# Two heads at a time in two attentions: paired matmuls, weights scaled on GpSimd, gate sums spread by DMA

## The chip, the cores and the metric

The kernel runs on one core of a Trainium2 chip. The metric is the device time of one execution in microseconds (us), taken as the median of several runs. The engines are named as the profile names them: PE (TensorE matmuls), PEld (its weight loads), DVE (VectorE), ACT (ScalarE), POOL (GpSimd), SP (SyncE, which issues all DMAs here).

## The reference

A token sequence of 256 rows of 1024 goes through two blocks: a first one of two layers (a mixer and a squared-ReLU MLP each) and a second one of one hybrid layer (SwiGLU, attention and state-space mixer, SwiGLU). The change touches the mixers of the first block's two layers only.

Layer 0 (called "even" in the kernel): 8 heads of block attention and 8 heads (2 groups of 4) of an attention with three branches, compressed keys, selected keys and window, that are weighted with gates and added. At 256 tokens both kinds of selection cover all keys, so each head is a causal softmax with a bias that depends on the distance:

```python
s = einsum('hqd,hkd->hqk', q, k) * 64**-0.5 + bias[h, bucket(t_q - t_k)]
o = einsum('hqk,hkd->hqd', masked_softmax(s, t_k <= t_q), v)     # nsa heads: g1 * slc + g2 * win + g0 * cmp
```

Layer 1 ("odd"): 16 heads of an attention with a forgetting gate:

```python
log_f = log_sigmoid(fz + b_forget)
cum = cumsum(log_f, axis=1).transpose(0, 2, 1)                   # per head
s = einsum('bhqd,bhkd->bhqk', qc, k) * scale + cq[..., None] - cum[:, :, None, :]
p = masked_softmax(s, key_pos[None, :] <= t[:, None])
o = einsum('bhqk,bhkd->bhqd', p, v)
```

## The kernel before

**Weights.** All weights come as a stream of 1 MB chunks from HBM in the order of use (`fetch_to`, issued by SP into three buffers RAW). ACT rounds a chunk to its high part WH (`hi_to`, L572), DVE subtracts to get the low part WL (`lo_to`, L580), and PE multiplies with both. `sp_gemm`, `act_gemm`, `dve_gemm` walk the products of the network in one fixed order, about two chunks ahead of PE. Every engine has its own hand-written program; semaphores join them. SP may load a RAW buffer again once WL of the chunk three places back is made.

**One attention step.** Layer 0 has 24 softmax passes over heads (8, then 8 selected and 8 window passes; called heads here), layer 1 has 16. Each engine runs a loop over i, and the stages of one head lie on different steps:

- PE, step i: the scores of head i (`pe_even_scores` L1363 and L1364, `pe_odd_scores` L1650 to L1659): queries in two tiles of 128, the first against 128 keys, the second against 256, so 384 columns in one PSUM bank. A head has 64 channels, so this product uses 64 of the 128 partitions; even heads lie on partitions 0 to 63, odd heads on 64 to 127. In layer 1 the gate's sums (`o_ln`, SPL, `trir`) and the causal mask are added by further matmuls into the same bank.
- DVE, step i: in layer 0 one custom instruction per query tile adds the bias from `e_bt` and finds the maximum (`dve_max_biased`, L909, L910). In layer 1 two plain maxima (L925, L926) and two small operations with the sums CQ (L1596, L1598).
- ACT, step i: exponential with row sum (`act_exp_biased` L899, L900, or `act_exp` L889, L890) into PB, four buffers.
- DVE, step i+1: reciprocal of the row sum (L934), and PB times it, in layer 0 times the gate too (`dve_weigh`, L941, L943).
- PE, step i+2: three transposes of PB (`pe_turn`, L879) into bank 5 or 6. ACT, step i+2: copy to PT, three buffers (`act_turned`, L918), which waits for the value product of the head before.
- PE, step i+3: the value product (`pe_pv`, L947, L948): 128 keys against the head's 64 columns of v, so output partitions 0 to 63 for even heads and 64 to 127 for odd ones. In layer 0 L1393 adds the compressed branch.
- After two heads (four in the later part of layer 0) ACT and DVE write the output rows as high and low part (`act_out` L953, `dve_out` L957) for the output product eo or oo, which follows at once.

PE issues in the order of its program: in step i scores of i, transposes of i-2, values of i-3. Two chunks of eo (at ACT steps 10 and 16, DVE steps 11 and 17) and of oo (5 and 10, 6 and 11) are split inside the loops.

**Around them.** In layer 0 the product ev1 stands in PE's program at step 2, the gates are computed on DVE at step 4, and four transposes of the compressed weights come at PE's step 6. In layer 1 the order of products is oq, ok, ov0, ov1 and then the attention; the gate's running sums are made by three small matmuls after ok and copied to CQ by DVE (L1584).

## Time and profile before

| what | value |
|---|---|
| median of 3 runs | 1335.26 us (1331.81 to 1339.88) |
| profiled execution, its own time | 1341.18 us |
| its span | 1339.4 us |
| PE busy | 1276.9 us, 95% |
| DVE busy | 859.8 us, 64% |
| ACT busy | 664.0 us, 50% |
| POOL busy | 197.1 us, 15% |
| attention of layer 0, after ev1 | 118.96 to 177.59, 58.63 us |
| attention of layer 1 | 456.96 to 505.60, 48.64 us |

Times are microseconds from the start of the span. The two last lines are stretches between instructions of PE: from its first score matmul after ev1 (or after ov1) to the first matmul of the output product. A matmul of two fp32 operands appears as two instructions ("x2"). Its end is modelled, so starts are the safer reading: what a matmul costs in a full queue is the distance from its start to the next start.

### The profile page before, as it was taken

The numbers are of one execution on the slowest core, as the hardware profiler recorded it, in microseconds if no ns is written. First come the engines' busy times: TensorE is split into PE (matmuls) and PEld (weight loads), VectorE is DVE, ScalarE is ACT, GpSimd is POOL, SyncE is SP. The second block draws the span as 40 slices with busy tenths as digits, with TensorE's granted clock in tenths as the row PEclk, the third lists the DMA queues.
The fourth block names the chain that finished last, engine by engine and source line by source line (L and its number), as shares of the span: only waits on it lengthen the run. The fifth ranks groups of instructions, "written<-read, shape, count | busy, mean of one in ns | idle before, by whom it ended". The sixth has DMA issues, their size and how long they took to land.

```text
span 1339.4 us, 19395 instructions
## 1 busy us (share of the span) xinstructions
PE 1276.9 (95%) x7812; PEld 1099.7 (82%) x7812; DVE 859.8 (64%) x1359; ACT 664.0 (50%) x1081; POOL 197.1 (15%) x224
## 2 busy tenths in 40 slices
PE   5999999999999999999999999999899889999996
PEld 5877578888888767888888888998897569888896
DVE  5864757666568376766557776547765665867643
ACT  5324646663333365665445554435544544655531
POOL 4000011120000001111111221101303401111201
PEclk8988999999999999999999999999899969999999
DMA  6590115555455212556554554562351005355461
GB/s 259 188 267 33 64 64 188 183 185 199 159 193 189 90 64 95 189 188 220 189 189 153 187 187 157 195 222 95 128 198 48 1 22 207 122 193 186 142 207 64
DMA packets 33913, 204.52 MB, mean 153 GB/s; under 512 B 3744, under 2 KB 6304, under 8 KB 13728
## 3 DMA queue, kind: packets, MB, share of 16 engines
q1 hardware_dynamic: 33824, 203.28, 43.9%
q8 instruction: 62, 1.02, 0.3%
q14 instruction: 27, 0.22, 0.1%
HBM read 201.82 MB, written 1.44 MB: 152 GB/s over the span
## 4 chain that ended last, share of the span: by engine, by line
PE 79%; DVE 12%; ACT 4%; DMA 2%; issue 1%; POOL 1%; SPq 1%; POOLq 0%; ACTq 0%; DVEq 0%
PE ps L636 32%; PE ps L641 22%; PE ps L639 6%; PE ps L640 6%; DVE wl L580 4%; PE ps L947 2%; PE ps L660 1%; PE ps L661 1%; PE ps L662 1%; DMA raw<-wstream 1%; ACT wh L572 1%; DVE xb L714 1%; ACT xb L694 1%; PE ps L948 1%; DVE y L1858 1%
## 5 line engine op out<-in xcount | busy, mean ns | idle before, releaser
L580 DVE TENSOR_TENSOR wl<-raw,wh 128x2048 fp32r<-128x2048 f32 (+3 forms) x201 | 435.6, 2173 | 149.4 <-ACT wh L572 148.8
L636 PE MATMUL ps<-xb,wh 128*128 128x512 f32 x1424 | 504.1, 399 | 4.6 <-DVE wl L580 3.5
L641 PE MATMUL ps<-xb,wl 128*128 128x256 f32 x1712 | 485.1, 283 | 0.0
L572 ACT ACTIVATE wh<-raw 128x2048 fp32r<-128x2048 f32 (+3 forms) x201 | 358.0, 1784 | 163.6 <-PE ps L641 124.3
L641 PEld LDWEIGHTS ps<-xb,wl 128*128 128x128 f32 x1712 | 328.8, 192 | 0.0
L636 PEld LDWEIGHTS ps<-xb,wh 128*128 128x128 f32 x1424 | 268.7, 189 | 71.4 <-issue 7.6
L641 PE MATMUL ps<-ab,wl 128*128 128x256 f32 x1088 | 307.6, 283 | 0.0
L636 PE MATMUL ps<-ab,wh 128*128 128x512 f32 x640 | 225.1, 397 | 2.7 <-DVE wl L580 2.7
L641 PEld LDWEIGHTS ps<-ab,wl 128*128 128x128 f32 x1088 | 207.6, 191 | 0.0
L636 PEld LDWEIGHTS ps<-ab,wh 128*128 128x128 f32 x640 | 120.2, 188 | 32.2 <-issue 2.2
L833 DVE TENSOR_TENSOR tf<-ps,tf 128x256 f32<-128x256 f32 x148 | 61.9, 421 | 118.2 <-ACT tf L828 118.2
L828 ACT ACTIVATE tf<-ps 128x256 f32<-128x256 f32 x148 | 56.3, 383 | 149.8 <-PE ps L641 148.2
L639 PE MATMUL ps<-ab,wh 128*128 128x256 f32 x448 | 128.3, 286 | 0.0
L640 PE MATMUL ps<-ab,wh 128*128 128x256 f32 x448 | 127.9, 285 | 0.0
L639 PE MATMUL ps<-xb,wh 128*128 128x256 f32 x288 | 85.4, 297 | 22.2 <-DVE wl L580 9.3
L724 POOL TENSOR_TENSOR acc<-acc,sq 128x256 f32<-128x256 f32 x42 | 30.7, 739 | 466.0 <-ACT sq L705 465.2
L639 PEld LDWEIGHTS ps<-ab,wh 128*128 128x128 f32 x448 | 86.5, 193 | 0.2
L640 PEld LDWEIGHTS ps<-ab,wh 128*128 128x128 f32 x448 | 86.5, 193 | 0.1
L1722 POOL TENSOR_TENSOR tf<-sg,tf 128x256 f32<-128x256 f32 x44 | 53.0, 1207 | 213.7 <-ACT sg L1687 213.7
L640 PE MATMUL ps<-xb,wh 128*128 128x256 f32 x288 | 84.3, 293 | 0.0
L639 PEld LDWEIGHTS ps<-xb,wh 128*128 128x128 f32 x288 | 58.2, 202 | 23.4 <-issue 9.9
L694 ACT ACTIVATE xb<-h,vecs 128x256 fp32r<-128x256 f32 x48 | 24.0, 508 | 78.9 <-DVE h L1471 37.6
(336 smaller groups left out, 1476.0 us busy)
## 6 DMA issues: line engine op xcount, KB each, us to landing
raw<-wstream SPq DMA_DIRECT2D x157, 1024.0 KB, 4.8
raw<-wstream SPq DMA_DIRECT2D x32, 704.0 KB, 4.1
raw<-wstream SPq DMA_DIRECT2D x8, 768.0 KB, 4.3
e_bt<-scratch SPq DMA_DIRECT2D x16, 128.0 KB, 6.3
raw<-wstream SPq DMA_DIRECT2D x2, 560.0 KB, 10.0
raw<-wstream SPq DMA_DIRECT2D x4, 256.0 KB, 5.6
h<-xt SPq DMA_DIRECT2D x4, 256.0 KB, 5.8
raw<-wstream SPq DMA_DIRECT2D x2, 512.0 KB, 7.7
```

Of the source, the lines that this page charges most:

```text
L572: e.g.activation(WH[i % HLN][:, 0:w], RAW[i % RAWN][:, 0:w], ACT.Copy).then_inc(S["hi"], 1)
L580: e.g.tensor_tensor(WL[q][:, 0:w], RAW[i % RAWN][:, 0:w], f32(WH[q][:, 0:w]), ALU.subtract).then_inc(S["lo"], 1)
L636: e.g.matmul(PS[b][:, :].rearrange("p (a t) -> p a t", a=2), wh[:, sl], x2[:, :, cs], start=start, stop=k == p.nk - 1, skip_group_check=pair)
L639: e.g.matmul(o, wh[:, sl], xh[:, cs], start=start, stop=False, skip_group_check=pair)
L640: e.g.matmul(o, wh[:, sl], xl[:, cs], start=False, stop=False, skip_group_check=pair)
L641: ins = e.g.matmul(o, wl[:, sl], xh[:, cs], start=False, stop=k == p.nk - 1, skip_group_check=pair)
L694: e.g.activation(XH[:, tile(k)], H[:, tile(k)], ACT.Copy, scale=gain(n, k)).then_inc(S["xh"], 1)
L724: e.g.tensor_tensor(acc, acc, SQ[:, mth * T:mth * T + T], ALU.add).then_inc(S["acc"], 1)
L828: e.g.activation(o, PS[p.bank[u]][:, T:2 * T], ACT.Copy).then_inc(S["low"], 1)
L833: return e.g.tensor_tensor(o, PS[p.bank[u]][:, 0:T], o, ALU.add)
L947: e.g.matmul(o[:, 0:256], v0, pt[:, 0:256], start=start, stop=False)
L1722: e.g.tensor_tensor(TF[j % 4][:, 0:T], SG[j % 2][:, :], TF[j % 4][:, T:2 * T], ALU.mult).then_inc(S["gp"], 1)
```

## The change

- Scores of two heads are issued together, in turn: the 128-column product of both, then the 256-column product of both. A fourth score bank (2) is added. PE issues them at odd steps, for heads i+1 and i+2.
- Value products of two heads are issued in turn, both into one bank, at even steps for heads i-4 and i-3. The banks of outputs are now two instead of three. In layer 0 the selected passes of both groups now come before the window passes of both.
- PB is scaled by POOL (`pool_weigh`) instead of DVE. DVE keeps the reciprocal.
- The copies of transposed weights are divided: even heads ACT, odd heads DVE (`dve_turned`). They wait for the value product three heads back instead of one.
- Layer 1: the running sums go as 16 rows of 256 into TMP, by DMA to a scratch in HBM, and come back by two DMAs that spread them over 128 partitions (`o_bt`, 1 MB each). DVE adds them with the maximum, as in layer 0. The matmuls of L1656 and L1659, and DVE's L1596 and L1598, go. SP waits for the sums before it issues the fetches of ov1.

```diff
+        o_bt = [place("o_bt0", 8 * T, at=ra), place("o_bt1", 8 * T, at=rl)]
...
+        def turned(j):
+
+            return (S["ptd" if j % 2 else "pt"], j // 2 + 1) if j < 40 else (S["pt"], j - 20 + 1)
...
-                e.wait_ge(S["pt"], j - len(A.TB) + 1)
+                e.wait(turned(j - len(A.TB)))
...
-            if i >= 3:
-                e.wait_ge(S["wt"], A.base + i - 3 + 1)
...
-            if j > A.pv_base:
-                e.wait_ge(S["pv"], j)
+            if j >= 3:
+                e.wait_ge(S["pv"], j - 3 + 1)
             e.g.activation(PT[j % 3][:, :], PS[A.turn_bank(q)][:, 0:384], ACT.Copy).then_inc(S["pt"], 1)
...
+        def dve_turned(e, A, q):
+            j = A.pv(q)
+            e.wait_ge(S["tp"], j + 1)
+            if j >= 3:
+                e.wait_ge(S["pv"], j - 3 + 1)
+            e.g.tensor_copy(PT[j % 3][:, :], PS[A.turn_bank(q)][:, 0:384]).then_inc(S["ptd"], 1)
+
+        def dve_reciprocal(e, A, q):
+
+            e.wait_ge(S["ex"], A.base + q + 1)
+            e.g.reciprocal(rs(q), sm(q)).then_inc(S["iv"], 1)
+
+        def pool_weigh(e, A, q, no, gate=None):
+            p, r = PB[q % 4], rs(q)
+            e.wait_ge(S["iv"], no + 1)
+            for tb, s in ((0, slice(0, 128)), (1, slice(128, 384))):
+                ins = e.g.tensor_scalar(p[:, s], p[:, s], r[:, tb:tb + 1], gate(tb) if gate else 1.0, ALU.mult, ALU.mult)
+            ins.then_inc(S["wt"], 1)
 
...
-        EVEN = Attention(0, 24, (3, 4, MISC), (5, 6), 0)
+        EVEN = Attention(0, 24, (3, 4, MISC, 2), (5, 6), 0)
...
+            for i in range(EVEN.n):
+                if i == 8:
+                    e.wait_ge(S["gated"], 2)
+                pool_weigh(e, EVEN, i, i, even_gate(i))
...
-                if 0 <= i - 2 < A.n:
+                if 0 <= i - 2 < A.n and i % 2 == 0:
                     act_turned(e, A, i - 2)
...
-            return d % 3
+            return d % 2
...
-                    dve_inverse(e, A, i - 1)
-                    dve_weigh(e, A, i - 1, even_gate(i - 1))
+                    dve_reciprocal(e, A, i - 1)
+                if 0 <= i - 2 < A.n and i % 2:
+                    dve_turned(e, A, i - 2)
...
+            pe_even_scores(e, 0)
             for i in range(A.n + 3):
...
+                    e.wait_ge(S["ol"], 1)
                     e.wait_ge(S["pct"], 2)
...
-                if i < A.n:
-                    pe_even_scores(e, i)
+                if i % 2 and i + 1 < A.n:
+                    pe_even_scores(e, i + 1)
                 if 0 <= i - 2 < A.n:
                     if i - 2 < 2:
...
-                if 0 <= i - 3 < A.n:
-                    pe_even_pv(e, i - 3)
+                if i % 2 == 0 and 0 <= i - 4 < A.n:
+                    pe_even_pv(e, i - 4)
...
+            if i == 2:
+                e.wait(G["even"].free.get(2))
+            if i >= 4:
                 e.wait_ge(S["mx"], i - 3 + 1)
...
+            for at, n in ((0, 128), (128, 256)):
+                for par in range(2):
+                    p_, ps = slice(64 * par, 64 * par + 64), PS[A.bank(i + par)]
+                    ins = e.g.matmul(ps[:, at:at + n], q[p_, qt + at:qt + at + 128], k[p_, kt:kt + n], start=True, stop=True)
+                    if at:
+                        ins.then_inc(S["sc"], 1)
...
-            if d < 3:
+            if d < 2:
                 e.wait(G["even"].free.get(b))
             else:
-                e.wait_ge(S["ol"], d - 3 + 1)
+                e.wait_ge(S["ol"], d - 2 + 1)
             if d == 2:
                 e.wait_ge(S["ptc"], 1)
-            e.wait_ge(S["pt"], q + 1)
-            pt = PT[q % 3]
+            for x in range(2):
+                e.wait(turned(q + x))
...
+                    for x in range(2):
+                        e.g.matmul(o[x][:, 0:256], e_vc[32 * j:32 * j + 32, 64 * x:64 * x + 64],
+                                   e_ptc[x][32 * j:32 * j + 32, :], start=True, stop=False)
...
+            for x in range(2):
+                e.g.matmul(o[x][:, 0:256], e_v[0][:, at[x]:at[x] + 64], pt[x][:, 0:256], start=start, stop=False)
+            for x in range(2):
+                e.g.matmul(o[x][:, 128:256], e_v[1][:, at[x]:at[x] + 64], pt[x][:, 256:384], start=False,
+                           stop=stop).then_inc(S["pv"], 1)
...
-        ODD = Attention(24, 16, (3, 4, MISC), (5, 6), 24)
+        ODD = Attention(24, 16, (3, 4, MISC, 2), (5, 6), 24)
 
         def sp_odd(e):
-            for name in ("on", "oq", "ok", "ov0", "ov1", "oo"):
+            for name in ("on", "oq", "ok"):
                 sp_gemm(e, G[name])
+            e.wait_ge(S["bt0"], 128)
+            e.wait_ge(S["bt1"], 128)
+            e.wait_ge(S["cq"], 1)
+            e.g.dma_start(bass.AP(scratch.tensor, 0, [[T, 16], [1, T]]), TMP[1][0:16, 0:T]).then_inc(S["d_scr"], 16)
+            sp_gemm(e, G["ov0"])
+            e.wait_ge(S["d_scr"], 32)
+            for i in range(2):
+                src = bass.AP(scratch.tensor, i * 8 * T, [[0, 128], [1, 8 * T]])
+                e.g.dma_start(o_bt[i][:, :], src).then_inc(S[f"ct{i}"], 16)
+            sp_gemm(e, G["ov1"])
+            sp_gemm(e, G["oo"])
...
-                    act_exp(e, A, i)
-                if 0 <= i - 2 < A.n:
+                    act_exp_biased(e, A, i)
+                if 0 <= i - 2 < A.n and i % 2 == 0:
                     act_turned(e, A, i - 2)
...
-            e.wait_ge(S["lf"], 1)
-            e.link(e.g.tensor_scalar(o_ln[:, :], o_lf[:, :], -1.0, None, ALU.mult))
-            e.settle()
-            e.link(e.g.tensor_copy(SPL[:, 0:16], o_ln[:, 0:16]))
-            e.settle()
-            e.g.tensor_tensor(SPL[:, 16:32], o_ln[:, 0:16], f32(SPL[:, 0:16]), ALU.subtract).then_inc(S["spl"], 1)
             dve_gemm(e, G["ok"], 0, drain=dve_to(G["ok"], o_k, 2))
             e.wait_ge(S["cum"], 1)
-            e.g.tensor_copy(CQ[:, 0:32], PS[MISC][:, 0:32]).then_inc(S["cq"], 1)
+            e.g.tensor_scalar(TMP[1][0:16, 0:T], PS[MISC][0:16, 0:T], -1.0, None, ALU.mult).then_inc(S["cq"], 1)
...
-                    cc, s = CQ[:, i:i + 32:16], SMALL[:, 64 + 2 * (i % 4):66 + 2 * (i % 4)]
-                    dve_max(e, A, i, last=False)
-                    e.wait_ge(S["cq"], 1)
-                    e.settle()
-                    e.link(e.g.tensor_tensor(s, cc, nm(i), ALU.subtract))
-                    e.settle()
-                    e.g.tensor_tensor(nm(i), cc, s, ALU.subtract).then_inc(S["mx"], 1)
+                    at = i % 8 * T
+                    e.wait_ge(S[f"ct{i // 8}"], 16)
+                    dve_max_biased(e, A, i, o_bt[i // 8][:, at:at + 128], o_bt[i // 8][:, at:at + T])
                 if 0 <= i - 1 < A.n:
-                    dve_inverse(e, A, i - 1)
-                    dve_weigh(e, A, i - 1)
+                    dve_reciprocal(e, A, i - 1)
+                if 0 <= i - 2 < A.n and i % 2:
+                    dve_turned(e, A, i - 2)
...
-            e.g.matmul(o[:, 0:16], c_("tri"), o_lf[:, 0:16], start=True, stop=True)
-            e.g.matmul(o[:, 16:32], c_("ones"), o_lf[:, 0:16], start=True, stop=False)
-            e.g.matmul(o[:, 16:32], c_("tri"), o_lf[:, 16:32], start=False, stop=True).then_inc(S["cum"], 1)
+            e.g.matmul(o[0:16, 0:128], o_lf[:, 0:16], c_("tri"), start=True, stop=True)
+            e.g.matmul(o[0:16, 128:256], o_lf[:, 0:16], c_("ones"), start=True, stop=False)
+            e.g.matmul(o[0:16, 128:256], o_lf[:, 16:32], c_("tri"), start=False, stop=True).then_inc(S["cum"], 1)
...
+            pe_odd_scores(e, 0)
             for i in range(A.n + 3):
-                if i < A.n:
-                    pe_odd_scores(e, i)
+                if i % 2 and i + 1 < A.n:
...
+                q = i - 4
+                if i % 2 == 0 and 0 <= q < A.n:
...
+                    b = d % 2
+                    if d < 2:
...
+                    for x in range(2):
+                        e.wait(turned(A.base + q + x))
+                    pts = [PT[(A.base + q + x) % 3] for x in range(2)]
+                    for s, v, c in ((slice(0, 256), 0, slice(0, 256)), (slice(128, 256), 1, slice(256, 384))):
+                        for x in range(2):
+                            ins = e.g.matmul(PS[b][64 * x:64 * x + 64, s], o_v[v][:, 64 * (q + x):64 * (q + x) + 64],
+                                             pts[x][:, c], start=v == 0, stop=v == 1)
+                            if v:
+                                ins.then_inc(S["pv"], 1)
...
-            ps, p_, t0 = PS[A.bank(h)], slice(64 * (h % 2), 64 * (h % 2) + 64), (h // 2) * T
-            e.wait_ge(S["ex"], 24 if h < 3 else A.base + h - 3 + 1)
-            e.wait_ge(S["cq"], 1)
-            e.wait_ge(S["spl"], 1)
-            e.wait_ge(S["const"], 1)
-            e.wait(G["ok"].done(3))
...
-            e.g.matmul(ps[:, 256:384], o_ln[:, 16 + h:17 + h].broadcast_to([128, 128]), c_("tri"), start=False, stop=False,
-                       skip_group_check=True)
-            for x in (h, 16 + h):
-                ins = e.g.matmul(ps[:, 0:384], SPL[:, x:x + 1].broadcast_to([128, 128]), trir[:, :], start=False,
-                                 stop=x > h, skip_group_check=True)
-            ins.then_inc(S["sc"], 1)
+            if h == 0:
+                e.wait_ge(S["ex"], 24)
+                e.wait_ge(S["cq"], 1)
+                e.wait_ge(S["const"], 1)
+                e.wait(G["ok"].done(3))
+            if h == 2:
+                e.wait(G["odd"].free.get(2))
+            if h >= 4:
+                e.wait_ge(S["mx"], A.base + h - 3 + 1)
+            t0, ps = h // 2 * T, [PS[A.bank(h + x)] for x in range(2)]
+            for at, n in ((0, 128), (128, 256)):
+                for x in range(2):
+                    p_ = slice(64 * x, 64 * x + 64)
+                    e.g.matmul(ps[x][:, at:at + n], o_q[p_, t0 + at:t0 + at + 128], o_k[p_, t0:t0 + n], start=at == 0,
+                               stop=False, skip_group_check=True)
+            for x in range(2):
+                for at in (0, 256):
+                    ins = e.g.matmul(ps[x][:, at:at + 128], identb[:, :], maskqb[:, :], start=False, stop=at == 256,
+                                     skip_group_check=True)
+                ins.then_inc(S["sc"], 1)
...
+            for i in range(ODD.n):
+                pool_weigh(e, ODD, i, 24 + i)
```

On PE in layer 1, about head 4 (`ps3` to `ps7` are PSUM banks, `o_k`, `o_q` keys and queries, `pb` the weights to transpose, `pt` the transposed ones, `o_v0` and `o_v1` the values of the first and second 128 tokens), before:

```order
L1650 MATMUL ps4<-o_k_119,o_q_118 128x128
L1652 MATMUL ps4<-o_k_119,o_q_118 128x256
L1654 MATMUL ps4<-maskqb_65,identb_64 128x128
L1655 MATMUL ps4<-maskqb_65,identb_64 128x128
L1656 MATMUL ps4<-consts_61,o_ln_123 128x128
L1659 MATMUL ps4<-trir_62,spl_80 128x384 x2
L879 MATMUL ps6<-consts_61,pb1_85 128x128 x3
L947 MATMUL ps2<-pt1_89,o_v0_120 64x256
L948 MATMUL ps2<-pt1_89,o_v1_121 64x128
```

The same place in the changed kernel, where the lines have moved to L1706 (scores), L1710 (mask), L884 (transposes) and L1684 (values):

```order
L1706 MATMUL ps7<-o_k_119,o_q_118 128x128
L1706 MATMUL ps2<-o_k_119,o_q_118 128x128
L1706 MATMUL ps7<-o_k_119,o_q_118 128x256
L1706 MATMUL ps2<-o_k_119,o_q_118 128x256
L1710 MATMUL ps7<-maskqb_65,identb_64 128x128 x2
L1710 MATMUL ps2<-maskqb_65,identb_64 128x128 x2
L884 MATMUL ps6<-consts_61,pb3_87 128x128 x3
L884 MATMUL ps5<-consts_61,pb0_84 128x128 x3
L1684 MATMUL ps1<-pt2_90,o_v0_120 64x256
L1684 MATMUL ps1<-pt0_88,o_v0_120 64x256
L1684 MATMUL ps1<-pt2_90,o_v1_121 64x128
L1684 MATMUL ps1<-pt0_88,o_v1_121 64x128
```

One head's nine rows have become twelve rows for two heads: two score products, two sets of transposes and two value products stand side by side, and no gate sums are among them.

On DVE in layer 1 before, one step (`nm` the maxima, `rs` the reciprocals, `sm` the row sums):

```order
L925 TENSOR_REDUCE nm_74<-ps7 128x1
L926 TENSOR_REDUCE nm_74<-ps7 128x1
L1596 TENSOR_TENSOR small_79<-cq_78,nm_74 128x2
L1598 TENSOR_TENSOR nm_74<-cq_78,small_79 128x2
L934 RECIPROCAL rs_76<-sm_75 128x2
L943 TENSOR_SCALAR pb1_85<-pb1_85,rs_76 128x128
L943 TENSOR_SCALAR pb1_85<-pb1_85,rs_76 128x256
```

In the changed kernel, a step with an odd number (5) and the first rows of the next:

```order
L912 ISA pb1_85,nm_74<-ps4,o_bt0_122 128x128
L912 ISA nm_74 128x1
L913 ISA pb1_85,nm_74<-ps4,o_bt0_122 128x256
L913 ISA nm_74 128x1
L963 RECIPROCAL rs_76<-sm_75 128x2
L958 COPY pt0_88<-ps6 128x384
L979 TENSOR_TENSOR ab_60<-ps0,ab_60 128x256
L581 TENSOR_TENSOR wl0_55<-raw0_49,wh0_52 128x2048
L912 ISA pb2_86,nm_74<-ps7,o_bt0_122 128x128
```

The scaling of PB is gone from DVE, and a copy that waits for PE's transposes (L958) now stands ahead of the next head's maximum, as do the output row (L979) and, at this step, a chunk's low part (L581).

On SP, the issues from ok to oo in the changed kernel (`raw` the weight buffers):

```order
L560 DMA raw_49<-wstream 128x2048
L1536 DMA scratch<-tmp_98 16x256
L560 DMA raw_50<-wstream 128x2048
L560 DMA raw_51<-wstream 128x2048
L1541 DMA o_bt_122<-scratch 128x2048
L1541 DMA o_bt_123<-scratch 128x2048
L560 DMA raw_49<-wstream 128x2048
```

The first row is ov0's second chunk, the next two weight rows are ov1's, and the last is oo's first. Before, the weight rows followed each other with nothing between them.

## Rows read from the trace of the kernel before

**Rows 1.** The page, busy time of PE, its share and instructions.

```profile
PE 1276.9 (95%) x7812; PEld 1099.7 (82%) x7812; DVE 859.8 (64%) x1359; ACT 664.0 (50%) x1081; POOL 197.1 (15%) x224
```

**Rows 2.** Windows: length, busy us (and count) by engine, TensorE clock, DMA share.

```profile
118.96:177.59 58.63, 55.24 (x278) 31.90 (x276) 40.17 (x180) 38.00 (x125) 0.00 (x0) 1.00 0.11 37
456.96:505.60 48.64, 46.33 (x274) 30.98 (x273) 31.64 (x121) 27.48 (x91) 0.00 (x0) 1.00 0.13 44
```

**Rows 3.** Timeline of PE, layer 0: start, length, what.

```profile
150.78 0.55 PE L879 MATMUL ps<-consts,pb 128*128 128x128 f32 x3
151.26 0.64 PE L1393 MATMUL ps<-e_ptc,e_vc 32*64 32x256 f32 x2
151.83 0.65 PE L947 MATMUL ps<-pt,e_v 128*64 128x256 f32 x2
...
152.62 0.49 PE L1363 MATMUL ps<-e_ks,e_qn 64*128 64x128 f32 x2
...
153.47 0.55 PE L879 MATMUL ps<-consts,pb 128*128 128x128 f32 x3
```

**Rows 4.** Timeline of PE, layer 1.

```profile
468.35 0.49 PE L1650 MATMUL ps<-o_k,o_q 64*128 64x128 f32 x2
...
469.20 0.23 PE L1654 MATMUL ps<-maskqb,identb 128*128 128x128 bf16 x1
...
469.33 0.44 PE L1656 MATMUL ps<-consts,o_ln 128*128 128x128 f32 x2
...
469.95 0.49 PE L879 MATMUL ps<-consts,pb 128*128 128x128 f32 x3
```

**Rows 5.** Timeline of PE, first two heads of layer 0.

```profile
108.64 0.59 PE L1364 MATMUL ps<-e_km,e_qm 64*128 64x256 f32 x1
...
108.84 0.56 PE L1363 MATMUL ps<-e_km,e_qm 64*128 64x128 f32 x1
...
109.41 1.06 PE L1364 MATMUL ps<-e_km,e_qm 64*128 64x256 f32 x2
110.39 0.60 PE L660 MATMUL ps<-wh,xb 128*128 128x280 f32 x1
```

**Rows 6.** Timelines of DVE and ACT, layer 0, start and length.

```profile
150.89 0.29 DVE L909 CUSTOM_DVE_ANT_0 pb<-ps,e_bt 128x128 f32<-128x128 f32 x1 [0.69 <-PE ps L1364]
...
151.57 0.40 ACT L899 ACTIVATE pb<-pb,nm 128x128 f32<-128x128 f32 x1 [0.49 <-DVE nm L910]
...
111.40 0.40 ACT L899 ACTIVATE pb<-pb,nm 128x128 f32<-128x128 f32 x1 [0.25 <-DVE nm L910]
...
112.42 0.17 DVE L934 RECIPROCAL rs<-sm 128x2 f32<-128x2 f32 x1 [0.49 <-ACT pb L900]
```

**Rows 7.** Single lines of POOL and ACT: count, ns min/median/max, first and last start.

```profile
L2033 POOL TENSOR_SCALAR tf<-m_u,vecs x12: 472/480/651, 928.1 to 957.2; 128x256 f32<-128x256 f32 x12
...
L1018 POOL CAST trir<-consts x3: 289/293/293, 28.8 to 29.3; 128x128 fp32r<-128x128 f32 x3
...
L918 ACT ACTIVATE pt<-ps x48: 465/487/517, 121.6 to 1089.7; 128x384 f32<-128x384 f32 x48
```

**Rows 8.** Timelines of ACT and DVE, chunk splits in layer 1.

```profile
469.83 1.93 ACT L572 ACTIVATE wh<-raw 128x2048 fp32r<-128x2048 f32 x1
...
472.07 2.28 DVE L580 TENSOR_TENSOR wl<-raw,wh 128x2048 fp32r<-128x2048 f32 x1
```

**Rows 9.** Before layer 1's attention: DVE, ACT, and all L559 fetches to landing.

```profile
435.68 0.18 DVE L1584 COPY cq<-ps 128x32 f32<-128x32 f32 x1
...
446.19 1.27 ACT L839 ACTIVATE o_v<-ps,rb 128x512 f32<-128x512 f32 x2 [3.46 <-PE ps L662]
...
DMA to landing us min/median/max: 1.8/4.8/11.7
```

**Rows 10.** Windows, as in Rows 2.

```profile
108.70:112.10 3.40, 3.40 (x16) 2.75 (x15) 2.75 (x15) 1.31 (x5) 0.00 (x0) 0.50 0.00 0
...
1064.40:1067.80 3.40, 0.85 (x5) 0.47 (x4) 3.31 (x7) 2.71 (x11) 2.16 (x3) 1.00 0.00 0
1067.80:1071.20 3.40, 3.40 (x11) 1.72 (x9) 0.24 (x2) 0.00 (x0) 2.12 (x3) 0.50 0.02 5
```

69 lines of the change are left out of this document (24 added, 45 removed).

## The prediction

> **What bounds the kernel now.** I read the page first: PE is busy for 95% of the span [rows 1], so a stage gets shorter only if PE's work or PE's waits there do. The windows of the two attentions come next: PE is busy for 55.24 of 58.63 us and for 46.33 of 48.64 us at the full clock, DVE for 40.17 and 31.64, ACT for 38.00 and 27.48, POOL not at all [rows 2]. Both stretches are PE's queue, and they are all that the change can shorten, 107.3 us in all. Third, the timeline of PE prices one head, from start to next start. Layer 0: transposes 0.48, compressed branch 0.57 (once for two heads), values 0.79, scores 0.85 [rows 3]; so 2.12 us a head without the branch and 2.69 with it. Layer 1: scores 0.85, masks 0.13, gate sums 0.62 [rows 4], with transposes and values 2.87 us a head. The reader is to see that nothing stands between these rows: each engine behind PE has slack.
>
> **What the change removes.** The gate sums go: 16 x 0.62 = 9.9 us of PE. The scores of two heads lie on different halves of the partitions. The trace has one place where two such products meet, the first two heads [rows 5]: head 1's 128 columns start at 108.84, 0.20 after head 0's 256 columns (108.64), and head 1's 256 columns start at 109.41. The clock is 0.50 there, 1.2 GHz [rows 10]. Head 1's 256 columns, alone, then take 0.98 us (109.41 to 110.39), so head 0's must have run from 108.64 to about 109.6, and head 1's 128 columns ran wholly beside them. Two halves do run at once. A pair therefore costs between 0.85 (all beside each other) and 1.70 (one after the other); I take 1.00, near the lower end, since the row shows a full overlap after 0.20 us. For value products, which split the output partitions and share all 128 input rows, no row shows two of them together: between 0.79 and 1.58 a pair; I take 0.95, by nearness to the scores. The Trainium skill (TensorE: Matmul & The Clock Gate, Part 3) states that column tiles run at once as row tiles do, with 2.38 times the rate for three; by it the value pair would be about 0.8 us, and rival B below would have no chance. No run here shows it, so B keeps one.
>
> **What PE then needs.** Layer 1, a pair: 1.00 + masks 0.26 + transposes 0.96 + values 0.95 = 3.17 us instead of 5.74. Layer 0: 2.91, and 3.24 where the branch comes (0.65 once in two pairs), instead of 4.24 and 4.81.
>
> **What waits instead.** With PE that fast I follow one round of the queues. DVE's copy of an odd head's transposed weights now stands ahead of the next head's maximum. From the start of the transposes of head h-3: transposes 0.50 with the handoff; copy 0.49 [rows 7]; output row, two thirds of that, 0.33; then head h's maximum, 0.68 from its start to that of the exponential (150.89 to 151.57) and 1.02 from there to the reciprocal (111.40 to 112.42) [rows 6]; reciprocal and handoff 0.22; POOL's scaling; then head h's transposes. POOL has no such instruction in the trace. The nearest rows are its tensor-scalar of 256 columns, 0.48, and its cast of 128, 0.29 [rows 7]: 0.77, and 0.87 with the handoff. Below this POOL can't go by any row; as upper end I take twice that, 1.5. Sum 4.11 us. Then PE does, in its order, head h's transposes, a value pair and a score pair (layer 1: 0.48 + 0.95 + 1.26 = 2.69) before the transposes of head h+1, with which the round repeats two pairs on. So two pairs take 6.80, a pair 3.40 us, a little more than PE's 3.17. In layer 0 the same sum, with the output row in half the rounds and the branch in half, gives 6.7, a pair 3.35. DVE (two maxima, two reciprocals, copy, row: about 2.3) and ACT (about 2.6) have room.
>
> **Chunk splits.** Each attention holds two: ACT 1.9 us, then DVE 2.3 us [rows 8]. Today PE's slack hides most. In the new round both engines are on the chain: the exponential, or the maximum behind the low part, comes late by the hi of 1.9 and the lo of 2.3 less gaps of about 1.3. I take 2.9 us of standstill for each of four splits; it is between 1 (hidden as now) and 4.2.
>
> **Layer 1.** Scores end at 456.96 + 1.26; first transposes 2.9 later, at 461.1; those of head 1 at 462.9 (0.48 + 1.26); head 15's seven pairs on, 486.7; transposes, copy and last value pair 2.1; splits 5.8: 494.6 instead of 505.60. **-11.0 us.** POOL, DVE and ACT here do everything beside PE. **Layer 0.** Up to head 6 the order is set by ev1, the gates on DVE (step 4) and the four transposes, now behind the first output row: 15.0 us today, 14.0 then. Eight periods 26.8, last pair 3.5, splits 5.8: 50.1 instead of 58.63. **-8.5 us.** The second score pair now ahead of ev1 only moves.
>
> **SP's queue.** The fetch of ov1's first chunk now stands behind the sums: DVE makes them at 435.7 [rows 9], with 256 columns instead of 32 until about 436.1, scratch write, issue at about 436.8, landing 4.8 later at the median, hi 1.8, lo 2.3: 445.7. PE needs it when ov0 ends, just before 446.19 [rows 9]. Cost 0; with the longest landing, 11.7, it is 6.5. I take 0.3. Behind it come ov1's second chunk (needed 5.5 us later) and the two 1 MB spreads; three more megabytes at 4.8 us each land by about 452 to 456, and DVE's first maximum needs them at 458.3: covered by ov1, but with 3 us or so to spare. What queues behind on SP is oo's first chunk, needed at step 5.
>
> **The clock.** After a stretch in which PE was busy 0.85 of 3.40 us the clock fell to half, 0.50 or 1.2 GHz [rows 10]. The four standstills of 2.9 us are of that kind. A pair under the lower clock takes twice PE's 3.17, 6.3 instead of 3.4 us: about 2.9 us for a fall that covers one pair. I take 2.4 falls (bounds 0 and 5): **+7.0 us**.
>
> **Sum.** -11.0 - 8.5 + 0.3 + 7.0 = -12.2 us against the profiled execution's 1341.18, so 1329.0. That execution was 5.9 us over the median of the runs (its span is 1339.4), so the median goes from 1335.3 to 1323.
>
> **Rivals.**
> A. The clock holds, or the splits hide better: -19 to -24 us, 1312 to 1316. For it: layer 0's loop is now at the full clock with PE busy for 94% [rows 2]. Against it: a standstill that in-order queues can't fill.
> B. Value products don't overlap: a pair costs 1.58, PE needs 3.80 (layer 1) and 3.87 and is the bound again; +0.45 us x 19 pairs = +8.6, less the standstills and falls that PE's new slack takes (-5): 1326 to 1327. For it: both products share input rows; no row speaks against it.
> C. Neither product overlaps (the pairing does nothing): a pair costs 4.50 in layer 1, 4.57 in layer 0. Layer 1 keeps most of the gate sums' 9.9, layer 0 gains about 2: 1326 to 1329. Against it: [rows 5].
> E. POOL is slow, 1.5 us a head: 0.73 more in every round of two pairs, 19 pairs x 0.37 = +7 us, 1330. The Trainium skill (SBUF — State Buffer, Who interferes with whom) says that a DVE operation with two SBUF inputs keeps GpSimd from reading. L580 is one, so a scaling would stand still for up to 2.28 us at each of four splits, +9 at most where it isn't already in the 2.9: 1332. No row in the groups decides it.
> F. ov1's chunk or the spreads land late: +3 to +7 us, 1326 to 1330.
> D. Slower. The clock stays at 1.2 GHz through most of both attentions, since the round is bound by a chain and PE idles in it again and again. Layer 1: 8 pairs x 6.3 and 8 us around them, 58 us, +10; layer 0: 14 + 8 x 6.5 + 7 = 73, +15: 1360. It decides from the point where falls eat the 19.5 us gained, seven of them. Against it: even so PE is busy for 3.17 of 3.40 between splits, where the row that fell had 0.85 of 3.40 [rows 10].
>
> **How the numbers follow.** Main case (about 1323, 1318 to 1328 by itself) 0.40, A 0.17, B 0.12, C 0.04, E 0.12, F 0.06, D 0.09. What the measurement can't tell from no change is 0.5%, 6.7 us. Faster by more (under 1328.6): nearly all of main, A, most of B, half of C and F, little of E: 0.72. Within it: most of E and the rests: 0.19. Slower: D, 0.09. The range leaves out D and the lower end of A: 1310 to 1335. Its lower end is all gains with no fall and splits that hide further; its upper end is E with its port waits, plus a late chunk.
>
> **What would show it.** The stretch from ev1's end to eo near 50 us plus falls, and that from ov1's end to oo near 38 plus falls (today 58.63 and 48.64). In PE's timeline score pairs with four starts in about 1.0 us, value pairs in about 0.95; between splits the transposes of odd heads 3.4 us apart and those of even heads preceded by a wait for POOL of some 0.2 to 0.6. POOL's scaling 0.77 us a head. Standstills of about 3 us after head 5 or 6, 10, 16, and the clock at 0.50 behind some. Wrong if value pairs take 1.6 (B), if POOL needs over 1.2 us a head (E), if PE waits at ov1 (F), or if the clock is low for more than 30 us of the two stretches (D).

## The result, and the profile after

The changed kernel takes 1324.85 us (median of 7 runs, 1321.5 to 1328.89) against 1335.26 us, of 7 runs too; the ratio is 0.9922, with a 95% interval from 0.9902 to 0.9942. Its profiled execution is the median one, 1324.85 us with a span of 1323.1 us. All times and ratios here and below are those of executions in the usual, faster state; two of e5's ten fell in the slower one (1351 and 1352 us) and are left out.

The page of the changed kernel, busy time by engine (answers to [rows 1]):

```profile
PE 1241.1 (94%) x7748; PEld 1075.5 (81%) x7748; DVE 840.8 (64%) x1296; ACT 655.7 (50%) x1061; POOL 236.5 (18%) x304
```

The windows of its two attentions, columns as in [rows 2]: length, busy time by engine, granted clock, DMA share.

```profile
117.54:173.97 56.43, 41.39 (x270) 24.53 (x268) 30.19 (x137) 31.69 (x113) 20.80 (x44) 0.82 0.11 38
453.64:490.74 37.10, 27.71 (x210) 17.58 (x209) 22.04 (x97) 25.09 (x83) 15.24 (x32) 0.86 0.16 57
```

Layer 1 went from 48.64 to 37.10 us, layer 0 only from 58.63 to 56.43 us (counted from its first score product, ahead of ev1, from 69.27 to 66.25). PE was busy for 94% and 95% of these stretches and now is for 73% and 75%: it waits. And the clock, 1.00 before, is 0.82 and 0.86.

PE's timeline in layer 0, a value pair and a score pair, and in layer 1 two rounds (start, length, what; in brackets the wait ahead and what ended it):

```profile
152.54 0.65 PE L1434 MATMUL ps<-pt,e_v 128*64 128x256 f32 x4
153.03 0.39 PE L1436 MATMUL ps<-pt,e_v 128*64 128x128 f32 x4
153.34 0.93 PE L1397 MATMUL ps<-e_ks,e_qn 64*128 64x128 f32 x8
154.20 0.55 PE L884 MATMUL ps<-consts,pb 128*128 128x128 f32 x3
157.56 0.55 PE L884 MATMUL ps<-consts,pb 128*128 128x128 f32 x3 [2.81 <-POOL pb L969]
...
480.60 0.55 PE L884 MATMUL ps<-consts,pb 128*128 128x128 f32 x3 [0.31 <-POOL pb L969]
481.07 0.87 PE L1684 MATMUL ps<-pt,o_v 128*64 128x256 f32 x8
481.87 0.93 PE L1706 MATMUL ps<-o_k,o_q 64*128 64x128 f32 x8
482.73 0.40 PE L1710 MATMUL ps<-maskqb,identb 128*128 128x128 bf16 x4
482.96 0.50 PE L884 MATMUL ps<-consts,pb 128*128 128x128 f32 x3
483.96 0.55 PE L884 MATMUL ps<-consts,pb 128*128 128x128 f32 x3 [0.49 <-POOL pb L969]
```

From start to start, a value pair takes 0.80 us (152.54 to 153.34) and a score pair 0.86 us (153.34 to 154.20): two heads in about the time of one in [rows 3]. The same even-head transposes come at 480.60 and, two pairs on, at 487.14: a pair in 3.27 us. These are the only two pairs of layer 1 with neither a split nor a low clock in them. The wait of 2.81 us is one of the standstills behind a split; the one behind layer 0's first split is 3.33 us, those in layer 1 are 2.03 and 1.45 us.

POOL's scaling (timeline of POOL; x2 is one head), with DVE's splits of layer 1 beside it:

```profile
481.93 0.83 POOL L969 TENSOR_SCALAR pb<-pb,rs 128x128 f32<-128x128 f32 x2 [1.39 <-DVE rs L963]
136.96 0.99 POOL L969 TENSOR_SCALAR pb<-pb,rs,e_v 128x128 f32<-128x128 f32 x2 [0.88 <-DVE rs L963]
476.89 3.65 POOL L969 TENSOR_SCALAR pb<-pb,rs 128x128 f32<-128x128 f32 x4 [3.77 <-DVE rs L963]
476.71 2.27 DVE L581 TENSOR_TENSOR wl<-raw,wh 128x2048 fp32r<-128x2048 f32 x1
```

A head costs 0.83 us, or 0.99 us with a gate. Only at 476.89 do two heads take 3.65 us and not 1.66: DVE's split had started 0.18 us before, and the longest scaling is 2334 ns against a median of 478, as the view of its line (ns min/median/max) says:

```profile
L969 POOL TENSOR_SCALAR pb<-pb,rs x48: 370/478/2334, 112.3 to 488.1; 128x128 f32<-128x128 f32 x24, 128x256 f32<-128x256 f32 x24
```

Windows of 3.4 us around layer 0's first split:

```profile
136.00:139.40 3.40, 2.68 (x22) 1.62 (x22) 2.19 (x7) 3.40 (x9) 1.07 (x3) 1.00 0.01 2
139.40:142.80 3.40, 0.66 (x3) 0.50 (x3) 3.40 (x16) 1.58 (x8) 1.28 (x3) 0.89 0.42 96
142.80:146.20 3.40, 3.40 (x20) 1.76 (x20) 0.32 (x3) 1.80 (x8) 1.69 (x4) 0.50 0.53 219
146.20:149.60 3.40, 3.39 (x22) 2.02 (x20) 1.58 (x9) 0.44 (x3) 0.30 (x1) 0.61 0.00 0
```

After the second of them, with PE busy for 0.66 of 3.40 us, the clock is 0.50 (1.2 GHz), as in [rows 10]. It falls five times in the two attentions: about 125 to 132, 142 to 149, 158 to 165, 459 to 463 and 470 to 476 us.

### The profile page after: what moved, and what is told of

The parts are those of the page before. It is cut to its first block, busy times and chain, and to the rows that moved or that the text cites. A ratio compares the mean times of both kernels' runs of the same rounds, so it can differ in the third digit from the quotient of the medians.

```text
span 1323.1 us, 19217 instructions
## 1 busy us (share of the span) xinstructions
PE 1241.1 (94%) x7748; PEld 1075.5 (81%) x7748; DVE 840.8 (64%) x1296; ACT 655.7 (50%) x1061; POOL 236.5 (18%) x304
## 4 chain that ended last, share of the span: by engine, by line
PE 80%; DVE 11%; ACT 4%; DMA 1%; POOL 1%; issue 1%; SPq 1%; POOLq 0%; DVEq 0%
PE ps L637 33%; PE ps L642 23%; PE ps L640 6%; PE ps L641 6%; DVE wl L581 3%; PE ps L661 1%; PE ps L663 1%; PE ps L662 1%; PE ps L884 1%; PE ps L950 1%; DMA raw<-wstream 1%; ACT wh L573 1%; POOL pb L969 1%; PE ps L1397 1%; DVE y L1909 1%
## 5 line engine op out<-in xcount | busy, mean ns | idle before, releaser
L581 DVE TENSOR_TENSOR wl<-raw,wh 128x2048 fp32r<-128x2048 f32 (+3 forms) x201 | 435.7, 2173 | 153.7 <-ACT wh L573 153.2
L695 ACT ACTIVATE xb<-h,vecs 128x256 fp32r<-128x256 f32 x48 | 24.0, 508 | 79.5 <-DVE h L1510 37.6
```

The source lines that it names most:

```text
L581: e.g.tensor_tensor(WL[q][:, 0:w], RAW[i % RAWN][:, 0:w], f32(WH[q][:, 0:w]), ALU.subtract).then_inc(S["lo"], 1)
L695: e.g.activation(XH[:, tile(k)], H[:, tile(k)], ACT.Copy, scale=gain(n, k)).then_inc(S["xh"], 1)
```

## The experiments

The table has for each kernel the two stretches of its profile (layer 0 from the first transposes to eo's first product, layer 1 from the first score product to oo's), the granted clock in each, their sum, and the sum less 0.3 us for each us at half clock, a price that e7 gives; so that column is an estimate. The time at half clock is twice (1 - clock) times the length. The ratio is that to the kernel before, with its interval.

```
kernel                layer 0       layer 1       sum     at full clock   ratio
before                57.68 (1.00)  48.60 (1.00)  106.28  106.3           1
changed               56.43 (0.82)  37.10 (0.86)   93.53   84.3           0.9922 [0.9902, 0.9942]
c1 changed, again     54.19 (0.87)  37.40 (0.91)   91.59   85.4           0.9880 [0.9827, 0.9934]
e1 split in pieces    47.28 (0.93)  33.29 (0.95)   80.57   77.6           0.9808 [0.9755, 0.9861]
e2 scaling on DVE     53.26 (0.87)  36.88 (0.91)   90.14   84.0           0.9865 [0.9820, 0.9910]
e3 values in a row    52.88 (0.90)  38.60 (0.82)   91.48   84.1           0.9858 [0.9816, 0.9899]
e4 scores in a row    57.47 (0.78)  38.91 (0.87)   96.38   85.8           0.9899 [0.9853, 0.9945]
e5 heads apart        57.21 (0.97)  37.86 (1.00)   95.07   94.0           0.9961 [0.9925, 0.9996]
e6 sums' work back    54.18 (0.87)  39.31 (1.00)   93.49   89.3           0.9928 [0.9905, 0.9951]
e7 waits filled       49.72 (1.00)  35.25 (1.00)   84.97   85.0           0.9896 [0.9851, 0.9942]
e8 reciprocal first   53.11 (0.90)  37.28 (0.86)   90.39   84.1           0.9903 [0.9874, 0.9932]
e9 e1 and e8          47.90 (0.93)  35.02 (0.92)   82.92   79.2           0.9869 [0.9836, 0.9902]
e10 e9, filled        48.89 (0.94)  34.62 (0.95)   83.51   80.7           0.9852 [0.9801, 0.9904]
e11 e1, filled        48.63 (0.93)  32.23 (1.00)   80.86   78.8           0.9813 [0.9777, 0.9849]
```

The times of the whole program carry a noise that has nothing to do with the change (last section), so the stretches decide.

**c1, the changed kernel again.**

> The changed kernel itself, unedited, beside the next three on one chip. Every theory expects its own time again, within 4 us of 1324.9, with four to six falls of the clock in the two attentions.

1321.39 us, span 1322.6: in layer 0 the waits are the same to 0.02 us (1.56, 1.85, 3.33 and 2.81); in layer 1 those behind the splits are 2.67 and 1.69 us in place of 2.03 and 1.45. The clock falls five times again, though partly at other places; it is low for some 21 us of the two stretches instead of 31, and their sum is 1.9 us less.

**e1, the splits in pieces.** The chunks' hi and lo parts, whole instructions of 2048 columns, become four of 512 (ACT: steps 7, 9, ... in layer 0 and 2, 4, ... in layer 1, behind the exponential; DVE: steps 9, 11, ... and 3, 5, ..., ahead of the copy):

```diff
-                if i in (11, 17):
-                    lo_to(e, G["eo"].first + (i - 11) // 6)
...
+                if piece(i, 9):
+                    c, x = piece(i, 9)
+                    lo_piece(e, G["eo"].first + c, x, c)
                 if 0 <= i - 2 < A.n and i % 2:
                     dve_turned(e, A, i - 2)
```

> The two chunk splits in each attention are cut into four pieces of 512 columns each, one piece every second head on ACT and on DVE, placed on DVE where it waits for PE's transposes. Theory (the splits stand the round still and the clock falls behind them): the long waits of PE for POOL's weights (3.33 and 2.81 us in layer 0, 2.03 and 1.45 us in layer 1) go, and with them the three clock falls that follow at 142, 158 and 470 us; layer 0 from 56.4 to about 50, layer 1 from 37.1 to about 33, the whole 8 to 11 us faster than the changed kernel (about 1315). Rival (a split is DVE work that lies on the round wherever it stands): the standstills turn into shorter ones in more rounds, and the time stays within 2 us of the changed kernel.

1310.32 us. PE's timeline of it in layer 0 where the changed kernel has its first standstill, and two rounds of layer 1:

```profile
137.92 0.55 PE L908 MATMUL ps<-consts,pb 128*128 128x128 f32 x3
138.93 0.55 PE L908 MATMUL ps<-consts,pb 128*128 128x128 f32 x3 [0.46 <-POOL pb L993]
...
452.06 0.55 PE L908 MATMUL ps<-consts,pb 128*128 128x128 f32 x3 [0.76 <-POOL pb L993]
455.68 0.55 PE L908 MATMUL ps<-consts,pb 128*128 128x128 f32 x3 [0.75 <-POOL pb L993]
```

No wait behind a split is left; the longest two, 1.85 and 1.78 us, are at the starts of the loops. The clock falls once in each stretch. 13.0 us less than the changed kernel in the stretches (11.0 less than c1; the forecast was 8 to 11), of which 7 to 8 stay at equal clock. The rival falls, though it has a part: a pair in layer 1 takes 3.62 us (452.06 to 455.68) and not 3.27. DVE's piece there waits for ACT's piece (0.35 us in each round), which was put one step ahead of it, and the copy stands behind it. Pieces of ACT further ahead should give this back; that was not tried.

**e2, the scaling on DVE.** In place of `dve_reciprocal`, and of `pool_weigh` on POOL:

```diff
-                    dve_reciprocal(e, A, i - 1)
+                    dve_inverse(e, A, i - 1)
+                    dve_weigh(e, A, i - 1, even_gate(i - 1))
```

> The scaling of the weights is put back on DVE (0.56 to 0.7 us a head there, against 0.83 to 0.99 on POOL and a handoff of about 0.2), all else as in the changed kernel. Theory (a round through DVE, ACT and POOL sets the pace): the chain gets shorter by some 0.5 us, but the next maximum waits behind the scaling and DVE has 3.5 us of work a pair, about the length of the round; so within 4 us of the changed kernel either way. Rival (POOL's slowness and its standstills under DVE's splits are what the change pays with): 6 us or more faster than the changed kernel. Rival the other way (DVE becomes the bound): 6 us or more slower.

1320.0 us; at equal clock the stretches are as long as the changed kernel's (84.0 against 84.3 and 85.4). The whole program can't tell the cases apart: it is 4.9 us under the changed kernel's first runs (8 by the ratios) and 1.4 under c1 (2 by the ratios), where the theory allowed 4 and a rival began at 6. DVE is busy for 43.01 of 53.26 us in layer 0, so it isn't the bound; waits behind the splits are 3.24 and 2.55 us there. In the stretches at equal clock, moving the scaling to POOL gained or lost no more than 1.4 us: by them the theory holds and both rivals fall.

**e3 and e4, one head's products after the other's.** For the values (and for the scores in the same way):

```diff
             for x in range(2):
                 e.g.matmul(o[x][:, 0:256], e_v[0][:, at[x]:at[x] + 64], pt[x][:, 0:256], start=start, stop=False)
-            for x in range(2):
                 e.g.matmul(o[x][:, 128:256], e_v[1][:, at[x]:at[x] + 64], pt[x][:, 256:384], start=False,
                            stop=stop).then_inc(S["pv"], 1)
```

> The value products of a pair are issued one head after the other (256 and 128 columns of the first, then of the second) and not in turn; a pair then takes about 1.58 us of PE instead of the measured 0.80. Theory (the round is a chain that holds one value pair and one score pair in two pairs of heads): 0.4 us a pair more from the chain, up to 0.8 where PE is then the bound: 19 pairs, 6 to 12 us slower than the changed kernel. Rival (the waits of PE hide it): within 2 us.

> The score products of a pair are issued one head after the other (128 and 256 columns of the first, then of the second) and not in turn; in turn a pair takes 0.86 us. Theory: the two still lie on different halves of the partitions, but a head's two products share a half, so only the last of the first head meets the first of the second: about 1.5 us a pair, 6 to 12 us slower than the changed kernel. Rival (order within the pair is free because two halves are told apart anyway, and PE's waits hide the rest): within 2 us.

1318.67 and 1324.45 us. PE's timeline of e3, one value pair (L1434 has the 256 columns of either head, L1435 the 128), rows of four windows within it:

```profile
132.20 0.44 PE L1434 MATMUL ps<-pt,e_v 128*64 128x256 f32 x2
132.47 0.39 PE L1434 MATMUL ps<-pt,e_v 128*64 128x256 f32 x2
132.68 0.40 PE L1435 MATMUL ps<-pt,e_v 128*64 128x128 f32 x4
133.01 0.38 PE L1397 MATMUL ps<-e_ks,e_qn 64*128 64x128 f32 x2
```

The program has first head 256, first head 128, second head 256, second head 128. The trace has all four passes of 256 columns (132.20 to 132.48) ahead of the four of 128 (from 132.68), and the pair takes 0.81 us as before. PE started the second head's product while the first head's second one waited for its half. e4's score pair takes 0.87 us, in turn it was 0.86:

```profile
134.68 0.93 PE L1397 MATMUL ps<-e_ks,e_qn 64*128 64x128 f32 x8
135.55 0.55 PE L884 MATMUL ps<-consts,pb 128*128 128x128 f32 x3
```

So these two didn't undo what they were meant to undo, and my theory for them was wrong. e4's stretches are 4.8 us longer than c1's, but with 35 us at half clock and not 21; at equal clock 0.4 us are left of it, and 1.5 against the changed kernel. The Trainium skill (TensorE: Matmul & The Clock Gate, Part 3, "The mechanism") says that weight loads may be pulled ahead, while products start and end in the program's order; for products on different halves this trace doesn't agree.

**e5, the heads really apart.** PE's order becomes score, transposes, score in odd steps and value, transposes, value in even ones.

```diff
-                    pe_even_scores(e, i + 1)
-                if 0 <= i - 2 < A.n: ... pe_turn(e, A, i - 2)
+                    pe_even_scores(e, i + 1, (0,))
+                if 0 <= i - 2 < A.n: ... pe_turn(e, A, i - 2)
+                if i % 2 and i + 1 < A.n:
+                    pe_even_scores(e, i + 1, (1,))
...
```

> In e3 and e4 the order within a pair made no difference: PE started the second head's products ahead of the first head's later ones. Here the three transposes of a head stand between the two score products of a pair, and between its two value products, so that they cannot meet. Theory (a pair costs half of two single heads, and the round's chain is only a little longer than PE's work): PE needs 1.65 us more a pair, 4.5 to 4.8 us in place of a round of about 3.6; 19 pairs at 0.8 to 1.2, so 15 to 22 us, less the standstills and the falls that disappear under PE's own work (5 to 8): 8 to 16 us slower than the changed kernel. Rival (the chain through DVE, ACT and POOL sets the pace whatever PE does, and the pairing is worth little): within 3 us.

1330.56 us (median of eight); its ratio, 0.9961 against c1's 0.9880, is 11 us more. Its waits for POOL in all of layer 0 (us in total, times, longest):

```profile
PE ps L884 <- POOL pb L969: 2.7, 2, 1.8
```

PE is the bound again (54.30 busy of 57.21 us) and the clock holds, so in the stretches only 3.5 us separate it from c1, under the 8 to 16 that I expected; at equal clock it is 9. This is where most of the pairing's gain went: of some 9 us, 5 to 8 were given back as falls of the clock (1.5 us are left against the changed kernel's profile, 3.5 against c1's). e5 is also case C as a kernel, the sums gone and nothing paired: 1330.6 us, where C had 1326 to 1329.

**e6, the gate sums' work back.** Zeros are added by products of the removed ones' shapes:

```diff
+                nil = SPL[:, 32:33].broadcast_to([128, 128])
+                e.g.matmul(ps[x][:, 256:384], f32(SPL[:, 32:33]).broadcast_to([128, 128]), c_("tri"), ...
+                for again in range(2):
+                    ins = e.g.matmul(ps[x][:, 0:384], nil, trir[:, :], start=False, ...
```

> PE adds zeros to each head's scores in layer 1 by products of the same shapes as the removed gate sums (0.62 us a head), while DVE still adds the spread sums; nothing else differs. Theory: a pair in layer 1 then needs 3.0 + 1.24 = 4.3 us of PE in place of a round of 3.4: layer 1 from 37.1 to 41 to 45, so 4 to 8 us slower than the changed kernel, not the full 9.9, since PE's waits take in the rest. Rival (the sums' whole time counts, as it did before the change, when PE never waited): 9.9 us slower. Rival (it hides in PE's waits): within 2 us.

1327.16 us, 5.8 over c1, though layer 0 is as in c1. Layer 1 is 39.31 us, PE busy for 33.23 of them, clock 1.00: 1.9 over c1 as measured, 4 to 5 at equal clock. Of the 9.9 us of PE's work, half hides in PE's waits and half of the rest in a clock that holds. Against my number of 41 to 45 the size is off, for the clock's sake; the rival of 9.9 falls; that of 2 us falls by the whole program and at equal clock, not by layer 1 as measured.

The two savings on PE don't add up. Against the kernel before, the stretches are 11.2 us shorter with the sums gone and no pairing (e5), 12.8 with the pairing and the sums' work kept (e6), and 12.8 to 14.7 with both (changed, c1). Once one of them has freed PE, the other mostly turns its work into waiting (PE is busy for 90.3 us of the stretches in e5 and for 65.5 in c1). The ratios of the whole program (0.9961, 0.9928, 0.9880 for c1) put them further apart.

**e7, the waits filled.** Products with no use, into the bank that the transposes then overwrite:

```diff
+            for x in range({2: 6, 3: 7, 10: 13, 16: 11, 24 + 5: 8, 24 + 10: 7}.get(j, 0)):
+                e.g.matmul(PS[b][:, 0:512], XH[:, 0:128], XH[:, 0:512], start=True, stop=True)
             e.wait_ge(S["wt"], A.base + q + 1)
```

> PE runs products with no use (512 columns, 0.23 us each, into the bank that the transposes then overwrite) where it stands still: 6, 7, 13 and 11 of them ahead of the transposes of the heads 2, 3, 10 and 16 in layer 0, 8 and 7 ahead of those of 5 and 10 in layer 1. No other work changes. Theory (the falls of the clock cost time of their own, besides the standstills ahead of them): the clock holds behind the filled waits and each fall that is gone gives back some 1.5 to 2.9 us: 5 to 10 us faster than the changed kernel. Rival (behind a standstill the chain through DVE, ACT and POOL sets the pace and a slow PE hides in it): within 2 us. Rival (the filler is in the way or the clock falls anyway): slower.

1323.01 us, with these windows of its two stretches:

```profile
120.69:170.41 49.72, 41.80 (x307) 26.68 (x306) 30.19 (x137) 31.70 (x113) 20.76 (x44) 1.00 0.13 44
450.52:485.77 35.25, 27.07 (x224) 17.64 (x223) 22.14 (x97) 24.87 (x83) 13.25 (x32) 1.00 0.17 61
```

The clock never falls in them, and they are 8.6 us shorter than in the changed kernel and 6.6 shorter than in c1. That is 0.28 (8.6 over 30.7) and 0.32 (6.6 over 20.8) us for each us at half clock. In layer 1 one thing more changes: POOL is busy for 13.25 and not 15.24 us, since no scaling falls under a split any more. In layer 0, where POOL does the same work in the same time, the price is 0.33 (6.7 over 20.3) and 0.32 (4.5 over 14.1), so it doesn't hang on that. The whole program is no faster: its profile lost the 6.6 us elsewhere, 3.7 of them in a stretch of long products that this edit doesn't touch (last section). In the timed runs the gain wasn't seen either (1323.0 against 1321.4, four runs each); whether more than chance stands behind that stays open.

**e8, the reciprocal ahead of the maximum.**

```diff
+                if i % 2 == 0 and 0 <= i - 1 < A.n:
+                    dve_reciprocal(e, A, i - 1)
                 if i < A.n:
                     ...
                     dve_max_biased(e, A, i, ...
```

> On DVE, in every even step, the reciprocal of the head before is put ahead of the next head's maximum; in the changed kernel it was ready when that maximum began and stood 0.56 us behind it, and POOL's scaling and PE's transposes waited for it. Nothing else differs from the changed kernel. Theory (the round is the chain PE, DVE, ACT, POOL; PE has slack): the clean rounds shrink from 3.2 to 3.8 us to about 3.0 to 3.4, with 14 such pairs some 4 to 6 us less in the two attentions, the standstills at the splits stay. Rival (PE or ACT's total work bounds the round): within 1 us.

1323.38 us, 84.1 at equal clock: nothing gained; by its time alone the rival (PE's or ACT's work is the bound) would do as well. The ring goes through the even head's maximum, not through the odd head's reciprocal, and the reciprocal, put ahead, makes that maximum later. ACT's timeline shows it where the pieces are in too, e9 and then e1 (the wait, 0.77 and then 0.60 us, is that for the even head's maximum, so ACT's work isn't the bound there):

```profile
460.71 0.40 ACT L926 ACTIVATE pb<-pb,nm 128x128 f32<-128x128 f32 x1 [0.77 <-DVE nm L937]
```

```profile
456.66 0.40 ACT L926 ACTIVATE pb<-pb,nm 128x128 f32<-128x128 f32 x1 [0.60 <-DVE nm L937]
```

**e9 and e10, e8 with the pieces, and filled.** Their edits are those of e1 and e8, and e7's fillers for the heads 2, 3 and 24 alone.

> Both edits: the splits in four pieces of 512 columns, and the reciprocal ahead of the maximum in even steps. In the run with the pieces a pair in layer 1 took 3.61 us with a wait of 0.75 us for POOL's weights in each. Theory: that wait shrinks to about 0.2, so the stretches come to about 44 and 31 us (47.3 and 33.3 with the pieces alone), 5 us less than with the pieces alone. Rival (a piece's 0.57 us on DVE is now the bound): within 1.5 us of it.

> As the run before, and PE runs 6, 7 and 7 products with no use ahead of the transposes of the heads 2 and 3 of layer 0 and 0 of layer 1, where it waits for the first weights. Theory (a fall of the clock costs what the slower round behind it adds, about 2 us each): the two falls left at 120 and 440 us go, 2 to 5 us less in the stretches than the run before. In the time of the whole program this may drown in the two paces of the long products elsewhere. Rival: no difference in the stretches.

1320.56 and 1318.88 us. Against the pieces alone the reciprocal ahead costs 1.6 us (79.2 against 77.6 at equal clock), a pair in layer 1 takes 3.8 us: a miss. e9's clock falls at 155, 445 and 472 us. In e10 only the fall at 445 is gone, the others come at 160 and 474 us, and the stretches are 0.6 us longer (83.51 for 82.92): a miss too.

**e11, the pieces, filled.** The pieces of e1 and these fillers:

```diff
+            for x in range({2: 6, 3: 7, 24: 7}.get(j, 0)):
+                e.g.matmul(PS[b][:, 0:512], XH[:, 0:128], XH[:, 0:512], start=True, stop=True)
```

> The splits in pieces, with the reciprocals where the changed kernel has them, and the products with no use ahead of the transposes of heads 2 and 3 of layer 0 and head 0 of layer 1. Theory: the stretches come to some 45 us and 32 us (47.3 and 33.3 with the pieces alone), since the two falls left there go; the whole then some 13 us faster than the changed kernel by the stretches, with 3 us to either side for the long products' pace. Rival (the fillers only move the falls): the stretches stay at 47 and 33.

1310.9 us. In layer 1 the clock holds and 1.1 us go; in layer 0 the fall moves from 121 to 156 us and the stretch is 48.6 us, 1.4 over e1's, where I expected 45: there the rival was right. The sum is e1's. The version that beats both kernels is e1, some 1.9% under the kernel before (two kernels with its pieces: 0.9808 and 0.9813).

## Why the prediction was right

**The sum.** Forecast 1323, measured 1324.85. On the profiled executions it was -12.2 us and came to -16.3: the one before lies 5.9 us over its median, as the prediction said, the one after on it. 14.6 of the 16.3 us are in the two attentions (3.0 and 11.5). Without falls (e7) the two stretches are 22.3 us under those before, where the prediction had 19.5.

**The products.** A score pair at 1.00 was 0.86 us, a value pair at 0.95 was 0.80. Cases B and C are out. The Trainium skill (TensorE: Matmul & The Clock Gate, Part 3) has column tiles run at once; the trace agrees, with 0.80 us for a pair against 0.79 for one head.

**The round.** Two pairs at 6.80 were 6.54 us in layer 1, in the one clean case. From the odd head's transposes (482.96) to the next even head's (487.14) it is 4.18 for my 4.11, PE's part 2.36 for 2.69. e2, e6 and e9 fit this ring and not an engine's load: work moved from POOL to DVE changed at most 1.4 us at equal clock, work added to PE came out at about half its size, and 0.17 us of DVE's work put ahead of the even head's maximum made a pair longer (3.62 to 3.8 us).

**The splits.** Forecast four standstills of 2.9 us, measured 3.33, 2.81, 2.03 and 1.45; e1 takes them away. So layer 0 without falls, forecast 50.1, is 49.7 (e7), and layer 1, forecast 37.6, is 35.3: the term for layer 1's splits, 5.8 us, was 2.3 us too high by the changed kernel's waits (3.5 together) and 1.4 by c1's (4.4).

**The clock.** Forecast 2.4 falls at 2.9 us, 7.0 us. Measured five at 1.7 us, 8.6 us (the changed kernel less e7). That the sum was near is luck: two errors met. The count was too low since I looked for falls behind the splits alone, and the first weights of each loop make PE wait as well. Rows of PE's timeline of the changed kernel, ahead of its falls at 125 and 459 us:

```profile
120.93 0.55 PE L884 MATMUL ps<-consts,pb 128*128 128x128 f32 x3 [1.56 <-POOL pb L969]
124.99 0.90 PE L884 MATMUL ps<-consts,pb 128*128 128x128 f32 x3 [1.86 <-POOL pb L969]
126.88 1.11 PE L1368 MATMUL ps<-consts,e_pc 128*128 128x128 f32 x4 [0.98 <-DVE ab L979]
457.87 0.52 PE L884 MATMUL ps<-consts,pb 128*128 128x128 f32 x3 [1.79 <-POOL pb L969]
```

The price was too high, most likely since a slow PE is partly hidden in waits that it would have had anyway (at 126.88 it waits 0.98 us within a fall), and since a pair needs less of PE than the 3.17 us that I took (2.84, from 480.60 to the end of the odd head's transposes): 0.3 us for each us at half clock, and not the 0.46 that I took (2.9 us for a pair that takes 6.3). This term is also why layer 0, forecast at -8.5 before the clock's share, came to -2.2: three falls, 6.7 us. The clock is low for 30.7 us of the stretches, just over the 30 that the prediction named as the mark of case D; the mark was wrong with the price, since 30.7 us cost 8.6.

**POOL.** Forecast 0.77 us, measured 0.83, with a gate 0.99. That a split keeps POOL from reading, which the Trainium skill states (SBUF — State Buffer, "Who interferes with whom"), happened once, and once in c1 (3.65 us for two heads); behind the other splits POOL had no scaling to do, since its reciprocal stood in DVE's queue behind the same split. Case E's 9 us came to 2, and its 1.5 us a head to 0.83.

**SP's queue.** Forecast 0.3 us; PE's timeline has no wait in ov0 or ov1, and DVE's first maximum (454.93) waited for PE, not for a spread. Case F is out.

## What to carry to other kernels

When an engine that bounds a stage gets less work, what bounds it next is a ring through all the queues. Follow one round from an instruction back to itself and look for the long instruction that stands in it now and then; cutting that into pieces was worth 11 to 13 us in the stretches, where in the changed kernel the pairing is worth 1.5 to 3.5 and the sums' removal some 2. Price the clock as a term of its own: look for PE's waits at a loop's start too, and take only part of the slower work as lost, here 0.3 us for each us at half clock. Where whole-program times scatter by 3 to 4 us, compare the stretches of the traces and the clock in them.

## What the runs showed of the hardware

**Products on different halves overtake.** See e3: the order within a pair makes no difference, only another product between them does (e5).

**Two paces at one clock.** In the long products PE starts either 115 or 117 to 118 products in 20 us, at a granted clock of 1.00 and with no wait. Windows of c1, then of e7, in the same product:

```profile
213.21:233.21 20.00, 20.00 (x117) 17.51 (x116) 11.68 (x14) 12.66 (x19) 4.17 (x4) 1.00 0.48 169
```

```profile
210.41:230.41 20.00, 20.00 (x115) 17.32 (x114) 11.79 (x14) 12.38 (x18) 4.17 (x4) 1.00 0.45 163
```

The pace holds through the whole of a long product, and is drawn anew for the next. From eo to layer 1's scores that makes 276.4 us (c1) or 279.7 us (changed kernel; 279.4 before). In the four longest such stretches (from about 220, 520, 720 and 1160 us) e3, whose total is low for its clock, had the fast pace each time (so had e4), and e2 the slow one in three. What sets it wasn't found.
